# Fourteen gates of a four-branch merge computed at other places: nine beside the state space branch, two beside the last dilated group, three beside the last stick-breaking head

## The chip, the cores and the metric

The kernel runs on 1 core of one Trainium2 chip. The metric is the device time of one execution in microseconds (us), as the median of several runs.

## The reference, cut to what matters

Two transformer blocks run one after the other over 1024 positions of width 1024, all in float32. The change is in the first one, in which four mixers read the same normed input `xn` and each is gated:

```python
xn = rmsnorm(x, attn_norm_g[l])
proj = xn @ w_in[l]
...
y_pool = pool_mixer(u_pool, pool_w[l], pool_scale[l])
y_dil = dilated_attention(qkv_dil, rel_bias)
y_sb = stick_breaking_attention(qkv_sb)
y_s5 = s5_mixer(u_s5, ...)
merged = jnp.zeros_like(x)
for bi, yb in enumerate((y_pool, y_dil, y_sb, y_s5)):
    gate = jax.nn.sigmoid(xn @ w_gate[l, bi])
    merged = merged + gate * (yb @ w_branch[l, row:row + width])
x = x + merged @ w_out[l]
```

A gate depends on `xn` alone, so it can be computed at any time after the norm. Stick-breaking attention needs, for each block of scores, a log-sigmoid (absolute value, exp and ln on ScalarE), a sum over the later keys, and an exp. The state space mixer (S5) needs a convolution inside blocks of 8 positions, a recurrence over 128 blocks with sines and cosines of its angles, a gelu, and a gated linear unit (GLU).

## The kernel before, in words

It is a bare program: each engine has its own instruction list, written out in functions that end in `_pe` (TensorE), `_act` (ScalarE), `_dve` (VectorE) and `_sp` (the DMA queue of SyncE), and they meet in semaphores (`wait_ge`, `give`, and `land` for a DMA).

**Products.** A float32 product is three passes in a reduced format: the high part of the weight by the high part of the input, high by low, low by high. One product makes a tile of 128 output features by 1024 positions. `product_steps` issues it in `kt` steps of 6 matmuls of 128x512 (L417), one step for each 128 rows of the contraction; `kt` is 8 where the input is `xn`, 4 for the GLU and for most branch outputs, 2 for the dilated output. All products stand in one list, `PLAN`. With product i, SP issues the load of the weight of product i+5 (L370, which waits until the low part of weight i+2 is made), ACT makes the high part of weight i+2 (L377) and DVE its low part (L382), from rings of three buffers. Each engine must meet the products in the order of the list.

**Order of the first block.** Input and norm; S5; merge of branch 3 (S5); pool; merge of branch 0; dilated attention in three groups; merge of branch 1; stick-breaking attention in four heads; merge of branch 2; output product; FFN. A merge has for each of 8 feature tiles `ft` a gate product with a sigmoid on ACT (L1057) into a gate buffer, and a branch product (`w_br`), whose result DVE multiplies by the gate and adds into `merged`. The gate of tile ft+1 stands ahead of the branch product of tile ft. Gate (3,0) (branch 3, tile 0) is made inside S5 already.

**S5 (`s5_sp`, `s5_pe`, `s5_act`, `s5_dve`, L678 to L960).** DVE builds the kernel matrices, PE multiplies them (L727), ACT copies them to `Ks`, SP lays them out as the blocks of `Mk` with 8 DMAs (L694). Then come two halves, each of: transposes of the input tiles (L740), transposes of weights and the input products `bu`, a chain on DVE with two sines on ACT (L815, L817) up to the states `H` (L934), and two tiles `y`, each of 96 matmuls of 128x128 (L771, L773), copied by ACT (L823) and transposed (L435). At the end stand gelu, its split into high and low parts, and eight GLU products; the first of these is read by DVE in L947.

**Dilated attention and sticks.** A dilated group has 11 slots, with scores (L1298), values (L1311) and outputs (L1323). Groups 0 and 1 hold the two query products of the next group between their slots, as `side`; group 2 has no side. The results of the three groups go out and come back by DMA (L1487, `dR`) in `combine`, at the start of the merge of branch 1, after the gate products of tiles 0 and 1 and beside the first products of stick-breaking (w_in 22, 26, 30). A stick-breaking head runs over units of up to 512 columns: scores (L1602), on ACT absolute value, exp and ln (L1663, L1665, L1667), a cast of the high part (L1673), sums (L1610 to L1616), addition on DVE (L1778), exp (L1681, L1684), values (L1624). Heads 0 to 2 hold the three input products of the next head as `side`; head 3 has none. ACT preloads one table that serves both exp and ln ahead of the heads.

Of the kernel before, what the change touches and what calls it, by code (L numbers as in the profile page):

```python
# [14 lines left out]
T = 1024  # L15
# [66 lines left out]

def weight_plan():
# [17 lines left out]
    tiles("w_gate", [24], 8)  # L101
# [213 lines left out]
def build(nc, A, out, scr, spill, bsc):  # L315
    from contextlib import ExitStack
    ctx = ExitStack()
    with ctx:
# [363 lines left out]

        def s5_sp(sp):
# [6 lines left out]
            sp.e.dma_start(bsc, brow).then_inc(*land("bsc"))  # L690
            sp.wait_ge("s5_ks", 1, 1)
# [15 lines left out]
        def s5_pe(pe):  # L707
            ring = [0, 1]
            rows_ring = [0, 1]
# [3 lines left out]
            for g in range(3):  # L713
                ps = psum.take(pe, ring, f"bias{g}", ("bias_row", g))
# [3 lines left out]

            for hf in range(2):
# [10 lines left out]
            product(pe, ring, "w_in", 36, XN, ("s5_u", 2))  # L730

            for hf in range(2):
                for fl in range(2):
# [7 lines left out]
                    ins.then_inc(*give("s5_ut", f, 0))  # L741
                    ps = psum.take(pe, rows_ring, f"s5ut{f}1", ("s5_ug", f))
                    pe.wait_ge("s5_ua", f)
                    transposed(pe, ps, dst, 8, "s5_ut", f, 1)
                for n in range(2):
                    ps = psum.take(pe, rows_ring, f"s5wt{hf}{n}", ("s5_wT", hf, n))
                    pe.wait_ge("s5_w", hf, n)
                    transposed(pe, ps, work[n], 8, "s5_wt", hf, n)
                pbu = [psum.take(pe, (pA, pB)[n], f"s5bu{hf}{n}", ("s5_rot", hf)) for n in range(2)]
# [7 lines left out]
                if hf == 0:  # L757
                    product(pe, ring, "w_in", 37, XN, ("s5_u", 3))
                else:
                    product(pe, ring, "w_gate", 24, XN, ("gate", 3, 0))  # L760
                for fl in range(2):
# [14 lines left out]
                    ps = psum.take(pe, rows_ring, f"s5yt{f}", ("s5_yu", f))  # L776
                    pe.wait_ge("s5_yc", f, 1)
                    transposed(pe, ps, work[fl], 8, "s5_yt", f)
            for f in range(4):
# [3 lines left out]
        def s5_act(act):  # L783
# [6 lines left out]
            u_tile(1)  # L790
            for hf in range(2):
# [4 lines left out]
            u_tile(2)  # L796
# [2473 lines left out]
```

## Time and profile before

| | us |
|---|---|
| median of 3 runs | 3949.2 |
| lowest, highest of them | 3944.52, 3952.15 |
| the profiled execution, its own time | 3953.94 |
| its span from first to last instruction | 3952.1 |
| PE busy | 3650.9 (92%) |
| DVE busy | 1658.8 (42%) |
| ACT busy | 1126.9 (29%) |
| mean granted TensorE clock | 0.943 |

The span is cut in 40 slices on the page of the profile. PE is busy for nine tenths or more of most of them; the exceptions are the first four (input and S5, six tenths), one with the pool branch, some with dilated and stick-breaking attention, and some in the second block. A busy share of PE counts time at half clock as well; the granted clock is given beside it as a share of 2.4 GHz.

### The profile page before, as it was taken

The page shows a single profiled execution, that of the slowest core. Times are in us where ns is not written, and L with a number is a line of the kernel's source. Part 1 is how long each engine was busy: PE and PEld are TensorE (multiplying, and loading weights), DVE is VectorE, ACT ScalarE, POOL GpSimd, SP SyncE. Part 2 cuts the span into 40 slices and gives each one's busy share as a digit, 9 for nine tenths or more (in the row PEclk, how much of TensorE's full clock was granted, in tenths as well). Part 3 has the DMA queues.
Part 4 walks back from the last instruction along what each step waited for, and adds up shares of the span by engine and source line. Part 5 has one row for each costly group of instructions (what it writes and reads, how often), then busy time and mean ns, then how long its engine had stood idle before and what let it go on. Part 6 is the DMA issues. An engine that isn't in the chain of part 4 may idle for free.

```text
span 3952.1 us, 38673 instructions
## 1 busy us (share of the span) xinstructions
PE 3650.9 (92%) x16598; PEld 2948.7 (75%) x16598; DVE 1658.8 (42%) x2021; ACT 1126.9 (29%) x1563; POOL 25.2 (1%) x69
## 2 busy tenths in 40 slices
PE   6669999988999899999999979999988989999997
PEld 4558888776776588888888857788866778888785
DVE  6343342322454424333233364415763354444354
ACT  3122111333235522211111145413442151212122
POOL 0000000000000000000000000000000000000000
PEclk8669999997999899999999989999976999999998
DMA  2003232110320012111111102120011111111111
GB/s 93 14 6 107 86 107 84 43 43 29 126 78 25 8 48 96 47 50 47 50 42 54 40 30 99 54 80 28 1 38 69 38 38 48 48 48 44 52 38 53
DMA packets 74554, 210.60 MB, mean 53 GB/s; under 512 B 11640, under 2 KB 21624, under 8 KB 74368
## 3 DMA queue, kind: packets, MB, share of 16 engines
q1 hardware_dynamic: 74384, 208.14, 16.1%
q8 instruction: 131, 2.15, 0.2%
q14 instruction: 39, 0.32, 0.0%
HBM read 190.03 MB, written 16.89 MB: 52 GB/s over the span
## 4 chain that ended last, share of the span: by engine, by line
PE 82%; DVE 9%; ACT 6%; issue 1%; DMA 1%; SPq 0%; ACTq 0%; DVEq 0%
PE PS L417 69%; PE PS L429 3%; PE PS L2571 1%; PE PS L2583 1%; PE PS L773 1%; PE PS L1602 1%; PE PS L2913 1%; PE PS L1323 1%; PE PS L435 1%; DVE work L552 1%; PE PS L2910 1%; PE PS L771 1%; DVE GS L2995 1%; ACT dS L1372 1%; DVE xlo L451 1%
## 5 line engine op out<-in xcount | busy, mean ns | idle before, releaser
L417 PE MATMUL PS<-xhi,whi 128*128 128x512 f32 x3120 | 988.8, 398 | 51.3 <-DVE xlo L451 42.8
L417 PE MATMUL PS<-xlo,whi 128*128 128x512 f32 x3120 | 968.1, 392 | 0.0
L417 PE MATMUL PS<-xhi,wlo 128*128 128x512 f32 x3120 | 966.0, 391 | 0.0
L417 PEld LDWEIGHTS PS<-xhi,whi 128*128 128x128 f32 x3120 | 585.6, 190 | 192.0 <-issue 49.8
L417 PEld LDWEIGHTS PS<-xlo,whi 128*128 128x128 f32 x3120 | 590.1, 189 | 125.0
L417 PEld LDWEIGHTS PS<-xhi,wlo 128*128 128x128 f32 x3120 | 589.2, 189 | 124.8
L382 DVE TENSOR_TENSOR wlo<-raw,whi 128x1024 fp32r<-128x1024 f32 (+4 forms) x307 | 329.8, 1075 | 537.5 <-ACT whi L377 537.5
L377 ACT CAST whi<-raw 128x1024 fp32r<-128x1024 f32 (+4 forms) x307 | 284.3, 927 | 506.0 <-PE PS L417 489.8
L417 PE MATMUL PS<-fhi,whi 128*128 128x512 f32 x704 | 219.4, 393 | 8.5 <-DVE flo L451 8.5
L417 PE MATMUL PS<-flo,whi 128*128 128x512 f32 x704 | 218.2, 391 | 0.0
L417 PE MATMUL PS<-fhi,wlo 128*128 128x512 f32 x704 | 218.1, 391 | 0.0
L417 PEld LDWEIGHTS PS<-fhi,whi 128*128 128x128 f32 x704 | 133.1, 190 | 37.7 <-DVE flo L451 10.2
L417 PEld LDWEIGHTS PS<-flo,whi 128*128 128x128 f32 x704 | 133.3, 189 | 28.0
L417 PEld LDWEIGHTS PS<-fhi,wlo 128*128 128x128 f32 x704 | 133.0, 189 | 27.9
L448 ACT CAST fhi<-fuv 128x1024 fp32r<-128x1024 f32 x44 | 46.1, 1048 | 328.6 <-DVE fuv L1993 222.0
L417 PE MATMUL PS<-yhi,whi 128*128 128x512 f32 x352 | 111.1, 397 | 9.3 <-DVE ylo L451 9.3
L417 PE MATMUL PS<-ylo,whi 128*128 128x512 f32 x352 | 109.8, 394 | 0.0
L417 PE MATMUL PS<-yhi,wlo 128*128 128x512 f32 x352 | 109.7, 393 | 0.0
L2076 DVE SCALAR_TENSOR_TENSOR merged<-PS,mod,merged 128x1024 f32<-128x1024 f32 x32 | 41.1, 1284 | 151.5 <-PE PS L417 151.5
L2060 DVE TENSOR_SCALAR fcb<-fsg,V 128x1024 f32<-128x1024 f32 x44 | 35.8, 814 | 163.8 <-ACT fsg L2036 163.8
L2000 DVE TENSOR_TENSOR merged<-PS,merged 128x1024 f32<-128x1024 f32 x32 | 39.2, 1225 | 137.7 <-PE PS L417 137.7
L2036 ACT COPY fsg<-PS 128x1024 f32<-128x1024 f32 x44 | 44.8, 1018 | 174.0 <-PE PS L417 174.0
(464 smaller groups left out, 3818.8 us busy)
## 6 DMA issues: line engine op xcount, KB each, us to landing
raw<-in_w_up SPq DMA_DIRECT2D x88, 512.0 KB, 3.3
raw<-in_w_in SPq DMA_DIRECT2D x67, 512.0 KB, 3.3
adr<-in_w_ada SPq DMA_DIRECT2D x48, 512.0 KB, 4.4
raw<-in_w_gate SPq DMA_DIRECT2D x32, 512.0 KB, 3.3
raw<-in_w_down SPq DMA_DIRECT2D x32, 384.0 KB, 3.1
raw<-in_w_down SPq DMA_DIRECT2D x32, 320.0 KB, 2.9
raw<-in_w_br SPq DMA_DIRECT2D x24, 256.0 KB, 2.7
spill<-wk SPq DMA_DIRECT2D x10, 512.0 KB, 4.8
```

Source lines behind the costliest of these rows:

```text
L377: act.e.copy(whis[i % RING][:, 0:kt, :], raws[i % RING][:, 0:kt, :]).then_inc(*give("w_hi", i))
L382: dve.e.tensor_tensor(wlos[i % RING][:, 0:kt, :], raws[i % RING][:, 0:kt, :], whis[i % RING][:, 0:kt, :].bitcast(F32), ALU.subtract).then_ ...
L417: ins = pe.e.matmul(ps[:, h * 512:(h + 1) * 512], w[s][:, k, :], x[:, h * 512:(h + 1) * 512], start=(at == 0 and n == 0), stop=(at == kt - ...
L429: ins = pe.e.matmul(ps[:, h * 512:(h + 1) * 512], ones, x[:, h * 512:(h + 1) * 512], start=first, stop=last)
L435: ins = pe.e.transpose(ps[:, j * 128:(j + 1) * 128], src[:, j * 128:(j + 1) * 128], ident)
L448: act.e.copy(dst, src).then_inc(*give(*signal))
L451: dve.e.tensor_tensor(dst, src, hi.bitcast(F32), ALU.subtract).then_inc(*give(*signal))
L552: dve.e.tensor_tensor(o, a, b, op).then_inc(*dve.step())
L771: pe.e.matmul(o, Ug[:, 2 * n + gl, :], Mk[:, 2 * i + gl, :], start=True, stop=False, skip_group_check=True)
L773: ins = pe.e.matmul(o, H[m][rows, n, :], CL[m][rows, i, 1:9, :].rearrange("p a b -> p (a b)"), start=False, stop=(m == 1), skip_group_chec ...
L2036: act.e.copy(GSG[v][:, FPAD:], psum.of(j)).then_inc(*give("f2_raw", v, i))
L2076: dve.e.scalar_tensor_tensor(X1[:, ft, :], psum.of(j), gt_f(ft), X1[:, ft, :], ALU.mult, ALU.add).then_inc(*give("f2_x", c, ft))
```

## The change

A table names fourteen gates that are computed ahead of their merges (one of them, (3,0), was early before). Nine of them, with the input products w_in 36 and 37, form one stream of 11 products or 88 steps in S5. The stream is cut into slots: 10 steps ahead of the kernel products, 3 and 6 around these, one after each group of transposes, 24 steps while DVE goes from `bu` to `H` in each half, one between each tile `y` and its transposes, and 5 ahead of the GLU. Gates (1,2) and (1,4) are the side of dilated group 2; gates (2,2), (2,4) and (2,0) the side of stick-breaking head 3. Twelve of the gates are stored to the DRAM tensor `spill` (from 18 to 50 tiles) and loaded again by SP in their merge; (3,0) and (2,0) stay. The merges skip the products of these gates. Addresses and PSUM banks move to make room, and the gelu of tile f waits for tile f alone.

```diff
+EARLY_S5 = ((3, 2), (3, 4), (3, 6), (0, 0), (0, 2), (0, 4), (0, 6), (1, 0), (3, 0))
+EARLY_DIL = ((1, 2), (1, 4))
+EARLY_SB = ((2, 2), (2, 4), (2, 0))
+RESIDENT = ((3, 0), (2, 0))
+EARLY = EARLY_S5 + EARLY_DIL + EARLY_SB
...
-            if ft < 8 and (b, ft) != (3, 0):
+            if ft < 8 and (b, ft) not in EARLY:
...
+    tiles("w_gate", [8 * b + ft for b, ft in EARLY_DIL], 8)
+    tiles("w_gate", [8 * b + ft for b, ft in EARLY_SB], 8)
...
+        BESIDE = [("w_in", 36), ("w_in", 37)] + [("w_gate", 8 * b + ft) for b, ft in EARLY_S5]
+        BESIDE0 = PLAN.index(("w_in", 36, 0, 8))
+        SLOTS = [("cl", 10), ("k", 3), ("ks", 6)]
+        for hf in range(2):
+            SLOTS += [(f"ut{hf}{fl}{x}", 1) for fl in range(2) for x in range(2)] + [(f"wt{hf}{n}", 1) for n in range(2)]
+            SLOTS += [(f"turn{hf}", 8), (f"sin{hf}", 8), (f"rot{hf}", 8)]
+            SLOTS += [(f"y{hf}{fl}", 1) for fl in range(2)]
+        SLOTS += [("glu", 8 * len(BESIDE) - sum(n for _, n in SLOTS))]
...
+        def beside_pe(pe):
+            def stream():
+                for p, (name, ft) in enumerate(BESIDE):
+                    done = ("s5_u", ft - 34) if name == "w_in" else ("gate", ft // 8, ft % 8)
+                    yield from product_steps(pe, [0, 1] if p % 2 == 0 else [1, 0], name, ft, XN, done)
+
+            steps = stream()
+
+            def slot(name):
+                for _ in range(dict(SLOTS)[name]):
+                    next(steps, None)
+            return slot
...
+        def beside_act(act, slot):
+            for kind, p in slot_events(slot, 6, 2):
+                name, ft = BESIDE[p]
+                if kind == "begin":
+                    begin_act(act, name, ft)
+                else:
+                    act.wait_ge("prod", BESIDE0 + p)
+                    if name == "w_in":
+                        act.e.copy(U[:, ft - 34, :], psum.of(BESIDE0 + p)).then_inc(*give("s5_u", ft - 34))
+                    else:
+                        if p == 2:
+                            act.wait_ge("s5_cl", 1)
+                        else:
+                            act.wait_ge("gate_out", *EARLY_S5[p - 3])
+                        act.e.activation(g_early, psum.of(BESIDE0 + p), ACT.Sigmoid).then_inc(*give("gate", ft // 8, ft % 8))
...
+        def beside_sp(sp, slot):
+            for kind, p in slot_events(slot, 0, 4):
+                name, ft = BESIDE[p]
+                if kind == "begin":
+                    begin_sp(sp, name, ft)
+                elif name == "w_gate" and p < len(BESIDE) - 1:
+                    sp.wait_ge("gate", ft // 8, ft % 8)
+                    sp.e.dma_start(spill[:, 18 + ft, :], g_early).then_inc(*land("gate_out", ft // 8, ft % 8))
...
+            beside_sp(sp, "cl")
+            beside_sp(sp, "k")
             sp.wait_ge("s5_ks", 1, 1)
             sp.wait_ge("s5_mzero")
             for q in range(8):
                 sp.e.dma_start(Mk[16 * q:16 * q + 16, :, 16 * q:128], Ks[:, :, 0:128 - 16 * q]).then_inc(*land("s5_mk", q))
-            begin_sp(sp, "w_in", 36)
-            begin_sp(sp, "w_in", 37)
-            begin_sp(sp, "w_gate", 24)
+            for name, _ in SLOTS[2:]:
+                beside_sp(sp, name)
...
-            rows_ring = [0, 1]
+            rows_ring = [2, 3]
...
-                if hf == 0:
-                    product(pe, ring, "w_in", 37, XN, ("s5_u", 3))
-                else:
-                    product(pe, ring, "w_gate", 24, XN, ("gate", 3, 0))
+                for x in ("turn", "sin", "rot"):
+                    beside(f"{x}{hf}")
...
+                    beside(f"y{hf}{fl}")
+                    ps = psum.take(pe, (pA, pB)[fl], f"s5yt{f}", ("s5_yu", f))
                     pe.wait_ge("s5_yc", f, 1)
                     transposed(pe, ps, work[fl], 8, "s5_yt", f)
...
-                act.wait_ge("s5_yu", 3)
+                act.wait_ge("s5_yu", f)
...
         def merge_pe(pe, b, ys, branch=None, beside=iter(())):
             def gate(ft):
-                product(pe, dense, "w_gate", b * 8 + ft, XN, ("gate", b, ft))
+                if (b, ft) not in EARLY:
+                    product(pe, dense, "w_gate", b * 8 + ft, XN, ("gate", b, ft))
...
-                dve.wait_ge("gate", b, ft)
+                dve.wait_ge("gate_in" if (b, ft) in EARLY and (b, ft) not in RESIDENT else "gate", b, ft)
...
+            def gate(ft):
+                if (b, ft) not in EARLY:
+                    begin_sp(sp, "w_gate", b * 8 + ft)
+                elif (b, ft) not in RESIDENT:
+                    if ft - 2 >= (1 if b == 3 else 0):
+                        sp.wait_ge("merged", b, ft - 2)
+                    else:
+                        sp.wait_ge(*clear)
+                    sp.wait_ge("gate_out", b, ft)
+                    sp.e.dma_start(gate_buffer(b, ft), spill[:, 18 + 8 * b + ft, :]).then_inc(*land("gate_in", b, ft))
...
+        def early_pe(pe, ring, gates):
+            for b, ft in gates:
+                yield from product_steps(pe, ring, "w_gate", 8 * b + ft, XN, ("gate", b, ft))
...
+        def early_act(act, gates, into, clear):
+            for n, (b, ft) in enumerate(gates):
+                i = begin_act(act, "w_gate", 8 * b + ft)
+                for _ in range(7):
+                    yield
+                act.wait_ge("prod", i)
+                act.wait_ge("gate_out", *gates[n - 1]) if n else act.wait_ge(*clear)
+                act.e.activation(into, psum.of(i), ACT.Sigmoid).then_inc(*give("gate", b, ft))
+                yield
...
+        def early_sp(sp, gates, into):
+            for b, ft in gates:
+                begin_sp(sp, "w_gate", 8 * b + ft)
+                for _ in range(8):
+                    yield
+                if (b, ft) not in RESIDENT:
+                    sp.wait_ge("gate", b, ft)
+                    sp.e.dma_start(spill[:, 18 + 8 * b + ft, :], into).then_inc(*land("gate_out", b, ft))
...
-                side = queries(side_ring, g + 1) if g < 2 else iter(())
+                side = queries(side_ring, g + 1) if g < 2 else early_pe(pe, side_ring, EARLY_DIL)
...
+            act.wait_ge("gate_out", *EARLY_DIL[-1])
...
-                side = qkv(h + 1) if h < 3 else iter(())
+                side = qkv(h + 1) if h < 3 else early_pe(pe, ring, EARLY_SB)
...
+            dve.wait_ge("merged", 1, 7)
...
-        SG[2] = [tile("sg", work_at + n * TB) for n in range(2)]
+        SG[2] = [sbv, tile("sg", work_at + TB)]
```

**SyncE's queue in S5.** Rows are DMAs in the order of issue. Before, from the copy of the bias rows on:

```order
L690 DMA bsc<-brow_102 4x1152
L694 DMA Mk_105<-Ks_107 16x4096
L694 DMA Mk_105<-Ks_107 16x32x112
L694 DMA Mk_105<-Ks_107 16x32x96
L694 DMA Mk_105<-Ks_107 16x32x80
```

And in the changed kernel:

```order
L767 DMA bsc<-brow_102 4x1152
L380 DMA raw_57<-in_w_gate 128x1024
L380 DMA raw_58<-in_w_gate 128x1024
L773 DMA Mk_105<-Ks_107 16x4096
L773 DMA Mk_105<-Ks_107 16x32x112
```

Two weight loads, which before stood behind all of the `Mk` DMAs, now stand ahead of them.

**TensorE at the end of the first tile `y` of the first half.** `CL` and `H` are the output matrices and states, `work_111` is the copied tile. Before:

```order
L771 MATMUL PS<-Mk_105,Ug_108 128x128
L773 MATMUL PS<-CL_103,H_116 128x128
L773 MATMUL PS<-CL_104,H_117 128x128
L435 MATMUL PS<-ident_50,work_111 128x128 x8
```

In the changed kernel:

```order
L852 MATMUL PS<-Mk_105,Ug_108 128x128
L854 MATMUL PS<-CL_103,H_116 128x128
L854 MATMUL PS<-CL_104,H_117 128x128
L427 MATMUL PS<-xhi_65,whi_61 128x512 x2
L427 MATMUL PS<-xlo_66,whi_61 128x512 x2
L427 MATMUL PS<-xhi_65,wlo_64 128x512 x2
L445 MATMUL PS<-ident_50,work_111 128x128 x8
```

One step of a gate product now stands between the tile and its transposes.

**ScalarE in the last stick-breaking head.** Rows of one unit, late in the head. Before:

```order
L1663 ACTIVATE sbt_148_196<-PS 128x512
L1665 ACTIVATE sbt_148_196<-sbt_148_196 128x512
L1667 ACTIVATE sbt_148_196<-sbt_148_196 128x512
L1673 CAST sbhi_194<-sbt_145_193 128x384
L1684 ACTIVATE sbt_140_188<-sbt_140_188 128x256
```

In the changed kernel, with the sigmoid of a side gate (L1235) behind the unit:

```order
L1804 ACTIVATE sbt_149_197<-PS 128x512
L1806 ACTIVATE sbt_149_197<-sbt_149_197 128x512
L1808 ACT_TABLE_LOAD
L1808 ACTIVATE sbt_149_197<-sbt_149_197 128x512
L1814 CAST sbhi_195<-sbt_146_194 128x384
L1825 ACT_TABLE_LOAD
L1825 ACTIVATE sbt_141_189<-sbt_141_189 128x256
L1235 ACT_TABLE_LOAD
L1235 ACTIVATE sbv_177<-PS 128x1024
```

Where no table was loaded inside a head before, one is now loaded ahead of each ln and each exp that follow the first sigmoid: 22 loads in this head.

## Rows read from the trace of the kernel before

**Rows 1.** The page: the chain that ended last, share by engine.
```profile
PE 82%; DVE 9%; ACT 6%; issue 1%; DMA 1%; SPq 0%; ACTq 0%; DVEq 0%
```

**Rows 2.** Busy time by stretch: stretch, us, PE, PEld, DVE, ACT, POOL busy, PEclk, DMA, GB/s.
```profile
134.30:157.60 23.30, 0.02 (x1) 0.05 (x1) 19.46 (x28) 2.91 (x3) 0.00 (x0) 0.57 0.00 0
157.60:193.50 35.90, 33.43 (x113) 26.14 (x114) 2.09 (x1) 2.15 (x4) 0.00 (x0) 0.50 0.00 1
331.80:453.00 121.20, 121.20 (x552) 100.90 (x551) 47.27 (x46) 23.85 (x27) 0.00 (x0) 1.00 0.36 119
930.50:973.70 43.20, 30.80 (x169) 27.24 (x169) 21.92 (x42) 18.56 (x74) 0.00 (x0) 0.57 0.10 22
1319.80:1372.90 53.10, 36.22 (x103) 19.88 (x102) 26.34 (x49) 30.28 (x63) 5.36 (x16) 0.81 0.00 0
```

**Rows 3.** Timeline, PE, two product starts in merge 3: start, us, engine, what.
```profile
331.75 0.62 PE L417 MATMUL PS<-xhi,whi 128*128 128x512 f32 x2
...
342.63 0.62 PE L417 MATMUL PS<-yhi,whi 128*128 128x512 f32 x2
```

**Rows 4.** The page: DMA issues, the spill stores, KB each and us to landing.
```profile
spill<-wk SPq DMA_DIRECT2D x10, 512.0 KB, 4.8
```

**Rows 5.** Timeline, SP's queue in S5: the eight DMAs of Mk.
```profile
93.80 13.11 SPq L694 DMA_DIRECT2D Mk<-Ks  x8
```

**Rows 6.** Timeline, DVE in S5; in brackets the idle time before and its releaser.
```profile
108.80 1.23 DVE L552 TENSOR_TENSOR work<-PR,Br 128x1024 f32<-128x1024 f32 x1 [12.78 <-DMA Mk<-Ks]
...
293.87 1.23 DVE L947 COPY U<-PS 128x1024 f32<-128x1024 f32 x1 [1.97 <-PE PS L417]
```

**Rows 7.** Timeline, PE in S5: the tiles y of both halves, first transposes.
```profile
157.58 0.77 PE L771 MATMUL PS<-Mk,Ug 128*128 128x128 f32 x2 [23.32 <-DVE H L934]
...
173.92 1.94 PE L435 MATMUL PS<-ident,work 128*128 128x128 f32 x8 [1.31 <-ACT work L823]
...
243.58 0.77 PE L771 MATMUL PS<-Mk,Ug 128*128 128x128 f32 x2 [24.39 <-DVE H L934]
```

**Rows 8.** Stretches in the second block, PE line L2901: us, PE busy, PEclk, DMA, GB/s.
```profile
2948.20:2952.80 4.60, 3.64 (x14) 1.00 0.00 0
2956.00:2972.00 16.00, 16.00 (x43) 0.50 0.00 0
```

**Rows 9.** Timeline, PE: start of dilated group 1, its end, end of group 2.
```profile
822.67 0.72 PE L1298 MATMUL PS<-K,Qs 64*128 64x128 f32 x8
...
878.35 1.21 PE L417 MATMUL PS<-xhi,whi 128*128 128x512 f32 x2 [0.52 <-DVE dO L1444]
...
973.69 1.22 PE L417 MATMUL PS<-xhi,whi 128*128 128x512 f32 x2 [0.52 <-DVE dO L1444]
```

**Rows 10.** Timeline, SP's queue, DVE and PE at the start of merge 1.
```profile
990.87 4.95 SPq L1487 DMA_DIRECT2D dR<-scr  x3
...
1004.45 0.19 DVE L552 TENSOR_TENSOR dM<-dR 128x32 f32<-128x32 f32 x1 [14.59 <-DMA dR<-scr]
...
1021.33 0.83 PE L417 MATMUL PS<-xhi,whi 128*128 128x512 f32 x2 [2.09 <-DVE wlo L382]
```

**Rows 11.** Timeline, PE: starts of stick-breaking heads 2 and 3.
```profile
1257.58 1.04 PE L435 MATMUL PS<-ident,sbv 128*128 128x128 f32 x8
...
1319.82 1.04 PE L435 MATMUL PS<-ident,sbv 128*128 128x128 f32 x8
```

**Rows 12.** Timeline, ACT: a table load in S5, two units of head 3, merge 2.
```profile
220.27 1.28 ACT L815 ACT_TABLE_LOAD   x1
221.56 1.06 ACT L815 ACTIVATE work<-work 128x1024 f32<-128x1024 f32 x1
...
1361.94 0.63 ACT L1684 ACTIVATE sbt<-sbt 128x512 f32<-128x512 f32 x1 [1.45 <-DVE sbt L1778]
...
1367.00 0.63 ACT L1684 ACTIVATE sbt<-sbt 128x512 f32<-128x512 f32 x1 [1.45 <-DVE sbt L1778]
...
1374.25 1.28 ACT L1057 ACT_TABLE_LOAD   x1 [0.28 <-DVE ylo L451]
```

More of the change, by code:

```diff
@@ L100, in weight_plan @@
     tiles("w_in", range(34, 38), 8)
-    tiles("w_gate", [24], 8)
+    tiles("w_gate", [8 * b + ft for b, ft in EARLY_S5], 8)
     tiles("w_glu", [x for i in range(4) for x in (i, i + 4)], 4)
@@ new lines, in build, with slot_events @@
+        SLOTS += [("glu", 8 * len(BESIDE) - sum(n for _, n in SLOTS))]
+        def slot_events(slot, begin_late, end_late):
+            at = 0
+            for name, n in SLOTS:
+                first, last = at, at + n
+                at = last
+                if name == slot:
+                    break
+            last = last if slot != "glu" else 1000
+            first = first if slot != "cl" else -1
+            events = [(8 * p + begin_late, "begin", p) for p in range(len(BESIDE))] + [(8 * p + 7 + end_late, "end", p) for p in range(len(BESIDE))]
+            return [e[1:] for e in sorted(events) if first <= e[0] < last]
@@ L708, in s5_pe @@
             ring = [0, 1]
-            rows_ring = [0, 1]
+            rows_ring = [2, 3]
+            beside = beside_pe(pe)
             pA, pB = [2], [3]
@@ L729, in s5_pe @@
                 ins.then_inc(*give("s5_kmm", hf))
-            product(pe, ring, "w_in", 36, XN, ("s5_u", 2))
+                beside("ks" if hf else "k")
             for hf in range(2):
@@ L744, in s5_pe @@
                     transposed(pe, ps, dst, 8, "s5_ut", f, 1)
+                    beside(f"ut{hf}{fl}1")
                 for n in range(2):
@@ L807, in s5_act @@
                     act.e.copy(WT[n], v8(psum.of(f"s5wt{hf}{n}"))).then_inc(*give("s5_wT", hf, n))
-                if hf == 0:
-                    u_tile(3)
-                else:
-                    i = begin_act(act, "w_gate", 24)
-                    act.wait_ge("prod", i)
-                    act.e.activation(g_early, psum.of(i), ACT.Sigmoid).then_inc(*give("gate", 3, 0))
+                    beside_act(act, f"wt{hf}{n}")
                 act.wait_ge("s5_turn", hf, 0)
@@ L890, in s5_dve @@
                 dve.e.tensor_tensor(wi, wi, wt, ALU.add).then_inc(*give("s5_w", hf, 1))
-                if hf == 0:
-                    begin_dve(dve, "w_in", 37)
-                else:
-                    begin_dve(dve, "w_gate", 24)
+                for fl in range(2):
+                    beside_dve(dve, f"ut{hf}{fl}0")
+                    beside_dve(dve, f"ut{hf}{fl}1")
+                for n in range(2):
+                    beside_dve(dve, f"wt{hf}{n}")
                 S, Cc, P, Q, R = work
@@ L1220, in build @@
         Vf = mem("Vf", y_at + 29184, [128, 2, T])
+        dil_gate = tile("dgate", y_at + 29184)
         Vt = mem("Vt", y_at + 37376, [128, 8, 256])
@@ L3128, in scalar @@
             sb_act(act)
[L3129 removed]
+            merge_act(act, 2, ("ysb_lo", 3, 1), done=merged_hi)
             out_act(act)
@@ L3150, in vector @@
             sb_dve(dve)
-            merge_dve(dve, 2, done=early_dve)
+            merge_dve(dve, 2, done=merged_lo)
             last_square = out_dve(dve)
```

80 lines of the change are left out of this document (54 added, 26 removed).

## The prediction

> **What bounds the kernel now.** I read the chain of waits first: 82% of the time that set the end is on PE, 9% on DVE, 6% on ACT [rows 1]. So most product time counts in full, but there are places where another engine leads. The busy time by stretch shows which [rows 2]. In merge 3 PE is busy for 121.20 of 121.20 us at full clock, with DVE at 47.27 and ACT at 23.85: a product less there is its whole time less. Three other stretches have room on PE. Before the first tile y of S5 PE does nothing for 23.3 us while DVE works for 19.46 of them. In dilated group 2 PE is busy for 30.80 of 43.2 us, in the last stick-breaking head for 36.22 of 53.1, in both partly at half clock (0.57 and 0.81 granted). The timelines then give the length of a product and the waits at the ends of these stretches.
>
> A gate product is 342.63 - 331.75 = 10.88 us at full clock, so a step is 1.36 us [rows 3].
>
> **The change part by part.** The sum is made against the profiled execution, 3953.9 us, which is 4.7 above the median of the runs.
>
> *Merges.* Gate (3,0) was early already, so 13 gate products leave the merges: 13 x 10.88 = 141.4 us less. Twelve loads of gates come in, with 4.8 us of flight for a tile of 512 KB as the stores have it [rows 4]. SP waits for the merge two tiles back before it issues one, and behind it queue weight loads for products five ahead, so they keep several products of cover. DVE and ACT keep their work and stay below PE: merge 3 becomes 121.2 - 3 x 10.9 = 88.6 us long with under 47.3 of DVE. I add 3 us for small stalls; bounds 0 (all covered) and 12 (1 us at each load).
>
> *S5, head.* SP issues two weight loads ahead of the eight `Mk` DMAs [rows 5]; the second waits for a low part that DVE makes in this stretch. DVE idles 12.78 us for `Mk` until 108.80 [rows 6], so a delay of `Mk` passes on. Bounds: 0, and one product period, 10.9. I take 5. From 108.80 to the last input product is 14.6 us before (157.58 - 23.32 - 10.88 = 123.4) [rows 7]; six single steps come in between transposes, of which most fall into waits of 1 to 2 us there. I add 2.6: `bu` ends at 131.0.
>
> *S5, the two stretches of 24 steps.* 24 x 1.36 = 32.6 us. Before, one product and the idle time behind it took 10.88 + 23.32 = 34.2 and 10.88 + 24.39 = 35.3 [rows 7]. DVE's chain hides under the steps; what PE's steps cost here is nothing, and they end a little before or with DVE. First tiles y at 163.6 instead of 157.6.
>
> *S5, tiles y.* A tile took 173.92 - 1.31 - 157.58 = 15.0 us at half clock [rows 7], with 33.43 of 35.9 us busy and a granted clock of 0.50 [rows 2]. PE now comes to them at full clock, from 32.6 us of dense products. Does it keep it? The nearest case is in the second block: small matmuls at 1.00 for 4.6 us, then 0.50 over 16.00 us in which PE was busy for 16.00 [rows 8]. So unbroken work of this kind did not hold the clock. I take the same: in the first 4.6 us at full clock 61% of a 7.5 us tile is done, the rest takes 5.8, so 10.4 for the first tile and 15.0 for the second; behind each one step (2.7 at half clock) and transposes (1.94). A pair: 10.4 + 15.0 + 2 x 4.7 = 34.8, against 35.9. The Trainium skill (TensorE: Matmul & The Clock Gate, Why this matters for your kernels) asks for no PE-idle gaps between bursts so that the clock stays up; by it the tiles would take 7.5 us each here, since PE has no gap before them. Rows 8 speak against that; it is rival B.
>
> *S5, to the end.* First pair ends at 198.4 (193.5 before). To the end of the second `bu` 14.6 us, plus 4.1 for six steps less the waits that they fill: 217.1; 24 steps: 249.7 (before 243.58); pair: 284.5; five steps, some at half clock, 8: 292.5, under which gelu and its split run; half a product, 5.4. The read of the first GLU product comes at 297.9 instead of 293.87 [rows 6]: **+4**. So the eight gates that are new here cost 4 us together.
>
> *Dilated group 2.* Group 1, with two side products, took 878.35 - 822.67 = 55.7 us, group 2 without them 43.2 [rows 9], which has 12.4 us of idle PE and a low clock. Two products are 21.8 us of PE at full clock: 30.8 + 21.8 = 52.6 if nothing ran faster, less what the higher clock gives back. I take 50: **+7** (bounds +4 and +12.5, the length of group 1).
>
> *Merge 1, head.* PE comes to product 30 at 1021.33, 47.6 us after the merge's start, with a wait of 2.09; DVE had waited 14.59 for `dR` and then worked 15.5 us on the combination before its weight parts [rows 10]. Without gate (1,0) PE is there at 36.8, but this chain does not shorten by itself. `dR` is issued at 17.2 us after the start now; I put it at 8 to 12, since ACT first waits for the last gate store (4.8 us [rows 4]). 10 + 13.6 + 15.5 + 1.4 = 40.5: **+4** of the 10.9 given back (bounds 0 and 10.9).
>
> *Stick-breaking head 3.* Three gates come in beside the units. Head 2, with three side products, took 1319.82 - 1257.58 = 62.2 us [rows 11], head 3 53.1: +9.1 by that alone. But a sigmoid replaces the table that held exp and ln, and the order shows 22 table loads after it where none was. A load is 1.28 us [rows 12]. ACT leads the units: 5.06 us each, with 1.45 idle, for DVE, before the last exp [rows 12]. The load ahead of that exp runs before the wait (as the load at 1374.25 ran ahead of its sigmoid's wait), so nine of them are hidden in 1.45 us each; if DVE were faster they would show. The eight ahead of ln and the five around the sigmoids are exposed: 13 x 1.28 = 16.6. Together 62.2 + 16.6 = 78.8: **+26** (bounds +9 with all hidden, +37 with all 22 exposed). The Trainium skill (ScalarE: Activation LUTs, What ACT_TABLE_LOAD costs) puts a switch at 2.66 us with a drain; by it 22 switches would be 58.5, the head 121 and the whole 29 us above case C. In the trace the sine follows its load at once (220.27 + 1.28 = 221.55, start 221.56), so I see no drain.
>
> *Moved addresses, banks, the gelu's wait for its own tile:* nothing; the DVE wait for the last tile of merge 1 stands before a memset whose work the first head needs only after it.
>
> Sum: -141.4 + 3 + 4 + 7 + 4 + 26 = -97.4, or 3856.5 for this execution; with 4.7 off for the median, **3852**.
>
> **The rivals.**
> *A, the forecast*, 3852, own range 3840 to 3866 by the bounds above taken together.
> *B, the clock holds in the tiles y.* Then a tile is 7.5 and step and transposes 2.4: a pair 19.8, 15 less, twice: 30 less, 3822. For it: PE has not one wait ahead of the tiles any more, and at 157.6 it came out of 23 us of nothing. Against it: rows 8.
> *C, all 22 loads exposed*: +37 instead of +26, 3863. For it: ACT already leads the units; against it: the waits of 1.45.
> *D, the clock is low through the dense steps of S5.* Waits on weights or on stores of gates (the next sigmoid waits for the store of the last, and PE's bank for that sigmoid) break the stream, and it runs at 1.2 GHz. A step is 2.72 then; 88 steps cost 120 us more, and the change is slower than before (3852 + 120 = 3972). It decides at 97.4 / 1.36 = 72 of 88 steps. Against it: merge 3 holds 1.00 with the same instructions and the same weight chain [rows 2].
> *E, the early gates stall their stages a little everywhere* (SP's queue in S5, PE waiting for a bank): 10 to 25 us, 3862 to 3877. The change does what it says: the order shows the gates at their new places.
>
> **How the numbers follow.** A 0.52, B 0.2, C 0.12, D 0.03, E 0.13. The likeliest is A: 3852. The range goes from a B with a little lost (3815) to E's end with C (3880). A measurement of this kernel can tell about 0.2% (8 us) from no change. All cases but D are faster by far more: faster 0.96, same 0.01, slower 0.03.
>
> **What would show it.** The granted clock in the two tile stretches (0.5 to 0.7: A; 1.0: B). PE busy without a break in two stretches of 32.6 us ahead of them. The `Mk` DMAs at 94 to 105. 22 table loads in head 3 and a length of 79 us, against 90 for C. Group 2 at 50. An idle of PE ahead of the third stick-breaking product in merge 1 of some 4 to 6 us. Merges with PE busy throughout. Wrong I would be most if head 3 or the tiles y came out otherwise, as they carry 26 and 30 us; if merges showed PE waiting for gate loads, the first term falls.

## The result, and the profile after

| | before | changed |
|---|---|---|
| median, us | 3950.16 (4 runs) | 3830.07 (4 runs) |
| lowest to highest | 3944.52 to 3952.15 | 3829.21 to 3833.62 |
| span of the profiled execution | 3952.1 | 3831.9 |
| mean granted clock | 0.943 | 0.964 |
| PE busy | 3650.9 (92%) | 3604.6 (94%) |

The ratio is 0.970, with a 95% interval of 0.9685 to 0.9714: 120 us faster. The forecast was 3852 with a range of 3815 to 3880, so the time is inside it, but 22 us under the value that was named, and the way there was partly another one.

The spans differ by 120.2 us. Set against each other at the same points of the two traces (ends of adds, of heads, of groups), they give:

| stretch | before, us | changed, us | difference | forecast |
|---|---|---|---|---|
| up to the read of the first GLU product | 293.87 | 276.15 | -17.7 | +4 |
| from there to the end of merge 3 (3 gates) | 162.67 | 130.05 | -32.6 | -32.6 |
| pool and merge 0 (4 gates) | 186.11 | 142.61 | -43.5 | -43.5 |
| dilated groups 0 and 1 | 235.18 | 233.17 | -2.0 | 0 |
| dilated group 2 with its products | 95.34 | 103.60 | +8.3 | +7 |
| merge 1 (3 gates) | 161.33 | 136.01 | -25.3 | -32.6 + 4 |
| stick-breaking heads 0 to 2 | 185.32 | 185.51 | +0.2 | 0 |
| head 3 | 53.0 | 80.4 | +27.4 | +26 |
| merge 2 (3 gates) | 133.13 | 100.49 | -32.6 | -32.6 |
| all behind it | 2446.1 | 2443.9 | -2.3 | 0 |

The ten gates of merges 3, 0 and 2 gave their full price, 10.88 us each, with no stall. The forecast had also 3 us for small stalls in the merges.

The busy time by stretch of the changed kernel, in the columns of [rows 2]: the first stretch of 24 steps in S5, the two pairs of tiles y, dilated group 2, the part of merge 1 from its first multiply on, and head 3.

```profile
128.40:161.20 32.80, 32.80 (x147) 27.16 (x146) 24.89 (x34) 8.71 (x9) 0.00 (x0) 1.00 0.28 79
161.19:182.94 21.75, 21.75 (x125) 16.78 (x123) 2.07 (x1) 3.08 (x5) 0.00 (x0) 1.00 0.07 28
235.31:256.91 21.60, 21.60 (x126) 17.09 (x125) 2.07 (x1) 4.40 (x7) 0.00 (x0) 1.00 0.00 1
834.90:885.58 50.68, 42.98 (x259) 34.77 (x258) 23.69 (x42) 24.92 (x79) 0.00 (x0) 0.93 0.13 40
944.29:1021.60 77.31, 72.13 (x318) 59.74 (x316) 46.46 (x47) 12.63 (x16) 0.00 (x0) 0.93 0.53 182
1207.10:1287.50 80.40, 65.79 (x246) 45.24 (x245) 29.58 (x52) 63.92 (x90) 5.42 (x16) 0.94 0.08 27
```

The largest surprise is in the second and third row: where the clock was 0.50 for 35.9 us [rows 2], it is now 1.00, and a pair takes 21.7 us instead of 36. PE has no idle time in it. Group 2 now takes 50.68 us; before, up to the same point, it was 42.7. In merge 1 a clock of 0.93 and 5.2 us of idle PE stand where it was 1.00. In head 3 ACT is busy for 63.92 of 80.40 us.

The timelines show the waits. On SP and DVE the start behind the `Mk` DMAs, with the columns of [rows 5] and [rows 6]:

```profile
70.17 28.14 SPq L380 DMA_DIRECT2D raw<-in_w_gate  x2
98.43 13.26 SPq L773 DMA_DIRECT2D Mk<-Ks  x8
```
```profile
113.46 1.23 DVE L562 TENSOR_TENSOR work<-PR,Br 128x1024 f32<-128x1024 f32 x1 [15.46 <-DMA Mk<-Ks]
...
276.15 1.23 DVE L1039 COPY U<-PS 128x1024 f32<-128x1024 f32 x1 [1.87 <-PE PS L427]
```

DVE goes on 4.66 us later than before (113.46 for 108.80), where 5 was forecast.

On PE: the first GLU product, the third stick-breaking product in merge 1, and the matmuls that finish the condition vector:

```profile
267.68 1.19 PE L427 MATMUL PS<-yhi,whi 128*128 128x512 f32 x2 [3.96 <-DVE ylo L461]
...
921.66 0.87 PE L427 MATMUL PS<-xhi,whi 128*128 128x512 f32 x2 [3.34 <-DVE wlo L392]
...
967.15 3.57 PE L1109 MATMUL PS<-ones,ada 128*128 128x1 f32 x16 [3.86 <-DVE ada L1085]
```

The first wait was 5.65 us before, but without five steps of other work ahead of it; the second was 2.09 [rows 10]; the third is new. All three leave PE at half clock for a while: a pair of 128x512 matmuls takes 1.19 us behind the first, for 0.62 at full clock [rows 3], and 1.05 and 1.20 behind the other two.

On ACT, one unit late in head 3:

```profile
1268.16 1.28 ACT L1808 ACT_TABLE_LOAD   x1
1269.45 0.64 ACT L1808 ACTIVATE sbt<-sbt 128x512 f32<-128x512 f32 x1
...
1270.61 1.28 ACT L1825 ACT_TABLE_LOAD   x1
1272.04 0.63 ACT L1825 ACTIVATE sbt<-sbt 128x512 f32<-128x512 f32 x1
...
1274.51 1.28 ACT L1808 ACT_TABLE_LOAD   x1
```

A unit takes 1274.51 - 1268.16 = 6.35 us, for 5.06 before [rows 12]: one load more, not two. The load ahead of the exp fills the former wait for DVE (1.45 us), as forecast. The ln starts right behind its load (1.29 us after the load's start, for 1.28 of load); this exp comes 0.15 us later, as its wait outlasts the load by that much. ACT's busy time in the head has 22 loads in it.

### The profile page after: what moved, and what is told of

Its sections match the earlier page's. It is cut to its first block, busy times and chain, and to the rows that moved or that the text cites. A ratio compares the mean times of both kernels' runs of the same rounds, so it can differ in the third digit from the quotient of the medians.

```text
span 3831.9 us, 38735 instructions
## 1 busy us (share of the span) xinstructions
PE 3604.6 (94%) x16598; PEld 2913.9 (76%) x16598; DVE 1658.3 (43%) x2021; ACT 1161.2 (30%) x1588; POOL 25.2 (1%) x69
## 4 chain that ended last, share of the span: by engine, by line
PE 83%; DVE 8%; ACT 7%; DMA 1%; issue 1%; SPq 0%; ACTq 0%; DVEq 0%
PE PS L427 69%; PE PS L439 2%; PE PS L2725 1%; PE PS L2713 1%; PE PS L3055 1%; PE PS L1743 1%; PE PS L445 1%; PE PS L3052 1%; ACT dS L1511 1%; PE PS L1462 1%; PE PS L1765 1%; PE PS L854 1%; DVE xlo L461 1%; DVE GS L3137 1%; PE PS L2718 0%
## 5 line engine op out<-in xcount | busy, mean ns | idle before, releaser
L392 DVE TENSOR_TENSOR wlo<-raw,whi 128x1024 fp32r<-128x1024 f32 (+3 forms) x307 | 329.9, 1076 | 471.2 <-ACT whi L387 471.2
L387 ACT CAST whi<-raw 128x1024 fp32r<-128x1024 f32 (+3 forms) x307 | 284.9, 929 | 514.6 <-PE PS L427 490.5
L427 PEld LDWEIGHTS PS<-fhi,whi 128*128 128x128 f32 x704 | 133.1, 190 | 37.7 <-DVE flo L461 10.2
L2202 DVE TENSOR_SCALAR fcb<-fsg,V 128x1024 f32<-128x1024 f32 x44 | 35.8, 814 | 163.6 <-ACT fsg L2178 163.6
```

The source lines that it names most:

```text
L387: act.e.copy(whis[i % RING][:, 0:kt, :], raws[i % RING][:, 0:kt, :]).then_inc(*give("w_hi", i))
L392: dve.e.tensor_tensor(wlos[i % RING][:, 0:kt, :], raws[i % RING][:, 0:kt, :], whis[i % RING][:, 0:kt, :].bitcast(F32), ALU.subtract).then_ ...
L427: ins = pe.e.matmul(ps[:, h * 512:(h + 1) * 512], w[s][:, k, :], x[:, h * 512:(h + 1) * 512], start=(at == 0 and n == 0), stop=(at == kt - ...
```

## The experiments

All are edits of the changed kernel, and are held against its 3830.1. The times of equal stages vary by some us from run to run: in merge 1 from its first multiply on, the unaltered code took 73.8 to 77.3 us in different kernels. Its traces show why. PE waits 2.85 to 3.86 us for the condition vector there; the clock falls at that wait each time, but it stays at half for 3.4 us in the traces with 73.8 to 74.0 us and for 6.8 to 10.2 us in the others. The program of the changed kernel gave both (77.3, and 73.8 in e11, which has the same instructions). Dilated group 2 with its products, 103.6 us in the changed kernel, took 98.8 to 104.2 with unaltered code. So a single stage is read from the traces, and a difference of a few us in these two is within what equal code does.

### Head 3: tables or TensorE

Run e1_raw_sb, where the sigmoid of the three gates (`RAW = EARLY_SB`) is taken in merge 2:

```diff
 # early_act, for the gates of head 3
...
-act.e.activation(into, psum.of(i), ACT.Sigmoid).then_inc(*give("gate", b, ft))
+if (b, ft) in RAW:
+    act.e.copy(into, psum.of(i)).then_inc(*give("gate_raw", b, ft))
+else:
+    act.e.activation(into, psum.of(i), ACT.Sigmoid).then_inc(*give("gate", b, ft))
...
 # merge_act, at the place of the gate
+if (b, ft) in RAW:
+    act.wait_ge("gate_raw" if (b, ft) in RESIDENT else "gate_in", b, ft)
+    act.e.activation(gate_buffer(b, ft), gate_buffer(b, ft), ACT.Sigmoid).then_inc(*give("gate", b, ft))
```

> The three gates beside stick-breaking head 3 are stored as plain products (a copy on ScalarE, which needs no table) and their sigmoids are taken in merge 2. No table is loaded inside head 3. Theory T (the table loads are what head 3 pays beyond the 62.2 us of a head with side products): head 3 falls from 80.4 to 62.2 us, time 3830 - 18 = 3812. Rival P (TensorE's side steps and the one PSUM pair that they share with the transposes hold the units back): head 3 stays at 75 us or more, 3825 or more. Merge 2 should not change under either.

Measured: 3810.85 us (ratio to before 0.9645, 0.9631 to 0.9660). Head 3 by stretch:

```profile
1199.60:1262.00 62.40, 59.33 (x246) 43.04 (x245) 29.45 (x52) 35.30 (x68) 5.34 (x16) 1.00 0.10 34
```

The same 246 matmuls take 62.4 us instead of 80.4, ACT's 63.92 us are 35.30, and the clock is 1.00 instead of 0.94. The 28.6 us of ACT that went are 22 x 1.28 with the difference of three copies. This is theory T; P is refuted. Merge 2 took 100.5 us as before the edit.

Run e2_preload puts the table back behind each sigmoid:

```diff
 act.e.activation(into, psum.of(i), ACT.Sigmoid).then_inc(*give("gate", b, ft))
+if b == 2:
+    act.e.preload_act_table_set("natural_log_exp_and_others")
```

> After each of the three sigmoids in head 3 the table that serves both exp and ln is loaded again; 6 loads instead of 22. Theory T with every load ahead of ln exposed: 8 x 1.28 = 10.2 us less, head 3 at 70, time 3820. If all of ScalarE's loads count once it is the busiest engine there, 16 x 1.28 = 20.5 less but not below 62.2 + 3 x 2.56 = 69.9, the same. Rival P: within 3 us of 3830.

Measured: 3820.98 us (0.9667, 0.9652 to 0.9681), head 3 at 73.2 us. The time is as T has it; the head is 3 us longer than the 70 that were expected. So the 16 loads that went are worth 7.2 us, not 10.2, and the six that are left beside the sigmoids cost 10.8 (73.2 - 62.4), more than the 7.7 us that they last.

Run e3_no_sb takes the three gates out of head 3:

```diff
-EARLY_SB = ((2, 2), (2, 4), (2, 0))
-RESIDENT = ((3, 0), (2, 0))
+EARLY_SB = ()
+RESIDENT = ((3, 0),)
```

> Undoes the three gates in head 3; all else as changed. The merge gets 3 x 10.88 = 32.6 us back, head 3 falls from 80.4 to 53.0 us (27.4 less): 5 slower than the changed kernel, 3835. If the gates cost something outside head 3 too (stores, the loads in merge 2), the time is under 3835; if they saved more than their products there, over it.

Measured: 3835.11 us (0.9704, 0.9688 to 0.9720). So three gates that save 32.6 us in merge 2 are worth 5 us with the sigmoids in the head, and 24 with the sigmoids left out of it (3835.1 - 3810.9).

### The clock in the tiles y

The trace of the changed kernel cannot tell whether the clock stays up because PE comes from dense products, or because of the step behind each tile. Three runs complete a table of two by two.

```diff
 # e4_gap: 8 of the 24 steps ahead of each pair are moved behind the tiles, ahead of the GLU
-            SLOTS += [(f"turn{hf}", 8), (f"sin{hf}", 8), (f"rot{hf}", 8)]
+            SLOTS += [(f"turn{hf}", 8), (f"sin{hf}", 8), (f"rot{hf}", 0)]
```

> The last 8 of the 24 steps ahead of the tiles y of each half are moved behind the tiles, to the slot ahead of the GLU. TensorE then idles some 7 us ahead of each pair of tiles. Theory G (the clock in the tiles is what TensorE brings with it; an idle time ahead of them loses it and the small matmuls don't win it back): granted clock 0.5 to 0.6 in the tiles, a pair 34 to 36 us instead of 21.7, time 3830 + 2 x 14 + 9.6 = 3868. Rival S (the step between the tile and its transposes holds the clock up, whatever was before): clock near 1.00, 2 x 4.1 us earlier at the tiles, 16 steps or 21.8 us later, 4 of them in an idle time: 3840.

Measured: 3855.42 us (0.9758, 0.9743 to 0.9772), between the two theories. The stretches are the first and the second tile of each pair, the timeline is PE's:

```profile
157.14:172.10 14.96, 14.96 (x48) 11.37 (x49) 0.00 (x0) 0.00 (x0) 0.00 (x0) 0.50 0.00 0
175.10:186.80 11.70, 11.70 (x64) 9.35 (x63) 2.06 (x1) 1.07 (x2) 0.00 (x0) 0.91 0.01 1
237.33:252.30 14.97, 14.97 (x49) 11.38 (x49) 0.00 (x0) 0.00 (x0) 0.00 (x0) 0.50 0.00 1
255.20:266.20 11.00, 11.00 (x65) 8.74 (x64) 2.07 (x1) 1.53 (x3) 0.00 (x0) 0.98 0.01 1
```
```profile
157.14 0.77 PE L852 MATMUL PS<-Mk,Ug 128*128 128x128 f32 x2 [6.88 <-DVE H L1023]
...
172.10 1.22 PE L427 MATMUL PS<-xhi,whi 128*128 128x512 f32 x2
...
185.13 0.74 PE L427 MATMUL PS<-xhi,whi 128*128 128x512 f32 x2
```

After 6.88 us of idle PE the first tile runs at 0.50 throughout, although PE is busy for all of its 14.96 us. The one step behind it begins at half clock (1.22), and behind step and transposes the second tile is at full clock, in the first pair after 0.6 us of it. Each theory had one half right.

```diff
 # e5_yout: the single steps behind the tiles are moved ahead of the GLU
-            SLOTS += [(f"y{hf}{fl}", 1) for fl in range(2)]
+            SLOTS += [(f"y{hf}{fl}", 0) for fl in range(2)]
```

> The four single steps between a tile y and its transposes are moved to the slot ahead of the GLU; the 24 dense steps ahead of each pair stay. Theory G (the tiles keep the clock that TensorE brings; 1.3 us of wait ahead of the transposes don't lose it): granted clock near 1.00 in both pairs, a pair 19 to 21 us, the end within 4 us of the changed kernel, 3826 to 3833. Rival S (only the steps in between hold it): the second tile of each pair at half clock, a pair 27 to 29, time 3842 or more.

Measured: 3843.14 us (0.9718, 0.9700 to 0.9737); of its four executions one was at 3830.38 and three at 3841.7 to 3848.3. Rival S. In the profiled one:

```profile
161.90:171.60 9.70, 8.46 (x49) 6.41 (x48) 0.00 (x0) 0.84 (x2) 0.00 (x0) 0.98 0.16 63
173.70:191.50 17.80, 16.64 (x57) 12.76 (x56) 2.09 (x1) 1.07 (x2) 0.00 (x0) 0.50 0.00 0
246.20:255.80 9.60, 8.41 (x49) 6.41 (x47) 0.00 (x0) 1.07 (x2) 0.00 (x0) 1.00 0.20 77
256.90:274.50 17.60, 16.44 (x56) 12.78 (x56) 2.10 (x1) 2.64 (x4) 0.00 (x0) 0.50 0.00 0
```

The first tile of each pair keeps the clock that PE brings, the second has lost it. The time of 3830.38 would fit an execution in which it was kept: its mean granted clock is 0.964, that of the other three 0.958 to 0.960. It has no trace.

Run e6_gap_yout has both edits.

> Both edits together: some 7 us of idle TensorE ahead of each pair, and no step behind a tile. In the run with the gap alone the first tile took 15 us at half clock and the second 8.4 at full, behind one step. If the clock comes back through that step, both tiles are at half clock here, a pair 34 to 36 us as before the change, and the time is some 5 us over the run with the gap alone (3855): 3860. If it comes back by itself in the transposes, a pair stays at 30 and the time at 3853.

Measured: 3877.93 us (0.9811, 0.9796 to 0.9825), 18 us over the expected 3860: the pairs came out as expected at half clock, but the second tiles, some 6 us longer in each pair, were left out of my sum. They are 12 of the 18 us; of the rest 3 lie between the pairs, and the others were not followed up.

```profile
156.20:192.20 36.00, 33.61 (x112) 25.94 (x112) 2.08 (x1) 2.15 (x4) 0.00 (x0) 0.50 0.00 1
245.05:281.00 35.95, 33.57 (x113) 26.26 (x114) 2.09 (x1) 4.05 (x6) 0.00 (x0) 0.50 0.00 0
```

These are the rows of the kernel before [rows 2]. So the table is:

| | no step behind a tile | one step behind each tile |
|---|---|---|
| 6.4 to 8.5 us idle ahead | half, half: 36.0 us | half, then full: 30 us |
| dense steps up to the tile | full, then half: 29 to 30 us | full, full: 21.7 us |

The two parts of the change that matter are the filled idle time and the single step. Each one alone leaves one tile of a pair at 1.2 GHz.

What the step does is not settled by that: it puts 128x512 matmuls behind the tile, and it also fills the wait ahead of the transposes, which in e5 is 1.53 and 1.22 us. The traces narrow it down. In the same execution of e5, later, PE waits as long behind 128x512 matmuls alone, and the clock stays at 1.00:

```profile
171.89 1.97 PE L445 MATMUL PS<-ident,work 128*128 128x128 f32 x8 [1.53 <-ACT work L906]
...
255.83 1.27 PE L445 MATMUL PS<-ident,work 128*128 128x128 f32 x8 [1.22 <-ACT work L906]
...
3213.01 0.73 PE L427 MATMUL PS<-fhi,whi 128*128 128x512 f32 x2 [1.46 <-DVE flo L461]
```
```profile
3211.50:3220.00 8.50, 7.04 (x32) 5.79 (x32) 4.24 (x4) 1.77 (x3) 0.00 (x0) 1.00 0.33 93
```

Over all traces there are 44 waits of 1.2 to 1.6 us behind a run of 128x512 matmuls alone, and the clock fell at one of them (in e10, 1002.29). And no tile that began at full clock lost it within its 8.4 us without a break. So the tile alone never took the clock and such a wait alone hardly ever; the wait behind the tile did in both pairs of e5. For the way back to full clock a filled wait is not enough: 15 us of tile without a break stayed at 0.50 (e4).

### The end of S5 and merge 1

Run e7_glu_order moves DVE's weight part behind the low parts of the gelu:

```diff
-            beside_dve(dve, "glu")
             for f in range(4):
                 dve.wait_ge("gx_hi", f)
                 lo_of(dve, Y[1][:, f, :], U[:, f, :], Y[0][:, f, :], "gx_lo", f)
+            beside_dve(dve, "glu")
```

> VectorE makes the low parts of the gelu's four tiles ahead of its weight part of the last slot, which waits for ScalarE's weight part behind all four gelus. Theory: the 3.96 us in which TensorE waits for the first GLU product go, and the half clock of its first matmuls with them: 4 to 5 us less, 3825.5. Rival (the gelu chain on ScalarE ends as late anyway): under 1.5 us less.

Measured: 3822.21 us (0.9668, 0.9653 to 0.9682). PE works on from the last transposes without a break, and the first multiply of merge 3 comes at 325.07 us instead of 330.55, 5.5 earlier. The medians differ by 7.9; the rest is not in this stage, and merge 1 from its first multiply on happened to take 74.0 us here.

Run e8_dil_26 takes another pair of gates for dilated group 2:

```diff
-EARLY_DIL = ((1, 2), (1, 4))
+EARLY_DIL = ((1, 2), (1, 6))
```

> The two gates beside dilated group 2 are (1,2) and (1,6) instead of (1,2) and (1,4); the number of products stays. Merge 1 gave back 8.5 us of the 21.8 that these two gates free from its first multiply on: TensorE waits 3.86 us for the condition vector that VectorE sums up, and goes on at half clock for a while. Theory V (VectorE has too much to do in the first half of this merge): the wait goes, 5 to 8.5 us less, 3822 to 3825. Rival D (the loads of gates and of the condition weights compete, whatever the place): within 2 us of 3830.

Measured: 3823.59 us (0.9674, 0.9658 to 0.9691), the time and the wait as theory V has them; D is refuted. From the first multiply of merge 1 on:

```profile
939.85:1009.17 69.32, 68.00 (x318) 56.51 (x317) 46.56 (x47) 12.62 (x16) 0.00 (x0) 0.99 0.55 191
```

With the same 318 matmuls, 69.3 us instead of 77.3 (73.8 to 77.3 with unaltered code), and no wait on `ada`. That is 90.5 - 69.3 = 21.2 of the 21.8 us of two gates. But V's reason, that DVE has too much to do, is not what the traces show. DVE has the same 46.5 us to do in both, and ends the eighth and last addition to the vector 22.8 us after the first multiply in the changed kernel and 22.0 here. In the changed kernel it even idles for 4.1 us on the way, 3.6 of them behind loads of condition weights, for example:

```profile
951.20 1.28 DVE L1085 SCALAR_TENSOR_TENSOR ada<-adr,cond,ada 128x1024 f32<-128x1024 f32 x1 [2.26 <-DMA adr<-in_w_ada]
...
965.81 1.28 DVE L1085 SCALAR_TENSOR_TENSOR ada<-adr,cond,ada 128x1024 f32<-128x1024 f32 x1 [1.11 <-DMA adr<-in_w_ada]
```

What moved is PE: it comes to the condition matmuls 19.0 us after the first multiply in the changed kernel, 30.3 us after it here, because the product of gate (1,4) stands ahead of them again and that of (1,6) is taken away behind them. A chain of some 22 us through DMA and DVE does not shorten with PE's products; whether DVE or the loads set its length was not tried.

Run e12_no_dil undoes the pair:

```diff
-EARLY_DIL = ((1, 2), (1, 4))
+EARLY_DIL = ()
-            act.wait_ge("gate_out", *EARLY_DIL[-1])
```

> Undoes the two gates beside dilated group 2; all else as changed. Two products come back to merge 1, 21.8 us; group 2 falls back by the 8 to 9 us that they cost it, and merge 1 loses its wait for the condition vector, 8.5 us less: 4 to 5 us slower than the changed kernel, 3834.5. If the wait stays although the gates are back, it is not theirs: 3843.

Measured: 3833.49 us (0.9704, 0.9690 to 0.9718). The wait is gone, and that part of merge 1 is at 90.5 us, as before the change. So the two gates were worth about 3 us as placed; this is within what runs differ by. With e8's choice they are worth 10 (3833.5 - 3823.6).

### A run that changed nothing, and the sum

Run e11_mk_first was to put the `Mk` DMAs ahead of one more weight load:

```diff
             beside_sp(sp, "cl")
-            beside_sp(sp, "k")
...
-            for name, _ in SLOTS[2:]:
+            for name, _ in SLOTS[1:]:
```

> In SP's queue the eight Mk DMAs go ahead of the weight load that waits for a low part; all else as changed. They start when the Ks copies end, 2.5 us earlier, and VectorE goes on 2.5 us earlier after them: 2 to 3 us less, 3827.5, if that chain sets the end there. If TensorE's steps set it (they fill 24 of 33 us without a break), nothing.

Measured: 3831.05 us (0.9695, 0.9681 to 0.9708), and no earlier `Mk`:

```profile
70.91 28.15 SPq L380 DMA_DIRECT2D raw<-in_w_gate  x2
99.18 13.62 SPq L772 DMA_DIRECT2D Mk<-Ks  x8
```

Both weight loads still stand ahead: they belong to the slot in front, and the slot that I moved holds none of SP's work. So this is the changed kernel once more, and says that two sets of runs agree within 1 us. What an earlier `Mk` would bring was not tried.

Run e9_all has e1, e7, e8 and that empty edit together.

> The four edits that point to a gain together: plain products stored beside head 3 (19 less by run e1), VectorE's order at the end of S5 (8 less by its median, 5.5 by the trace), gates (1,2) and (1,6) beside dilated group 2 (6.5), and the Mk DMAs ahead of one more weight load (2.5, not measured yet). If they add up: 3830 - 19 - 6 - 6.5 - 2.5 = 3796, give or take 3. If two of them share a wait: above 3802.

Measured: 3800.40 us (0.9618, 0.9605 to 0.9632). Without the 2.5 us of the `Mk` edit 3798.5 was expected: the three add up within the 3 us that were allowed. By the medians of the single runs (19.2, 7.9 and 6.5) they would have come to 3796.5. Head 3 took 62.33 us at clock 1.00, merge 1 from its first multiply on 68.7. This version beats the changed kernel by 29.7 us and the kernel before by 151.

Run e10_all_raw_dil adds the gates beside group 2 to those stored as plain products (`RAW = EARLY_SB + EARLY_DIL`).

> As the run before, and the two gates beside dilated group 2 are stored as plain products as well, with the sigmoid in merge 1. Three or four table loads of 1.28 us and the sigmoid's place leave group 2. Theory: 2 to 5 us less than the run before. Rival: in merge 1 ScalarE now waits for the load of the gate ahead of its weight parts, where a branch product lasts 2.7 us only, and TensorE waits behind it: 0 to 8 us more.

Measured: 3805.20 us (0.9632, 0.9618 to 0.9645), 4.8 more than e9: the rival. Merge 1 from its first multiply on took 72.8 us for 68.7, and PE has a wait for the condition vector again:

```profile
1002.29 1.92 PE L1109 MATMUL PS<-ones,ada 128*128 128x1 f32 x16 [1.56 <-DVE ada L1085]
```

Group 2 took 101.1 us for 101.9, a smaller difference than equal code shows from trace to trace, so this does not tell what its table loads cost. What holds the vector up in merge 1 (ACT's weight parts behind the load of a gate, as the rival has it) the trace does not single out.

## Why the prediction was right or wrong

*Merges: right to the tenth where PE alone led.* PE busy 121.20 of 121.20 us was all the evidence that was needed. "DVE and ACT keep their work and stay below PE" failed in merge 1: its branch products have two steps (2.7 us), and condition work is woven in, whose vector is ready 22.8 us after the first multiply, while PE, with a gate product less, comes to it after 19.0. I read the room from merge 3, whose branch products have four steps and which has no such chain, and carried it over. It gave back 7.3 us, where 4 at its head and a share of 3 were forecast; the head itself gave back nothing that can be seen (first multiply 11.4 us earlier, counted from the merge's first product, for 10.88 of gate), since `dR` was issued 6.2 us after the merge's start, not 8 to 12.

*S5: the step that failed is "I take the same: in the first 4.6 us at full clock 61% of a 7.5 us tile is done, the rest takes 5.8".* It cost 26 us of forecast: pairs of 34.8 were measured at 21.7 and 21.6. The reading under it was wrong: [rows 8] shows two stretches, at 1.00 and at 0.50, and "unbroken work of this kind did not hold the clock" skips what lies between them. There PE idled:

```profile
2952.80:2956.00 3.20, 0.75 (x2) 0.50 (x2) 3.00 (x6) 0.00 (x0) 0.00 (x0) 0.64 0.02 5
```
```profile
2955.25 17.92 PE L2901 MATMUL PS<-gv,kdt 64*128 64x256 f32 x44 [2.46 <-DVE GS L2995]
```

The clock fell in that wait of 2.46 us, not in unbroken work. It is the same order as in e5, where the first tile runs 8.4 us at 1.00 and the clock falls about the wait behind it, so that only the second tile is at half. I also had the step of dense matmuls behind each tile in hand, but priced it only as 2.7 us of work and gave it no effect on the clock. Rival B said 3822; the 8 us that lack to it are in S5 too (276.15 for the 267.9 that it gives for the read of the first GLU product): a pair is 21.7 and not 19.8, as a tile takes 8.4 us at full clock and not half of 15.0, and from the second pair to that read it is 19.2 us for 13.4, with the first GLU product waiting 3.96 us and running at half clock, which no case had. The cause of that wait is DVE's weight part ahead of the gelu's low parts (e7). S5 was forecast 21.7 us too long, which is nearly all of the 22 us between the named value and the median. That the other errors leave almost nothing is luck: 3 us of stalls did not come and the stages that nobody touched took 4.1 us less, while merge 1 took 3.3 us more than forecast, head 3 1.4 and group 2 1.3.

*The idle time that was filled* is a cause as well: e4 costs 25.3 us, of which the moved work accounts for the 9.6 that were worked out ahead of it; the two pairs together took 17 us longer. The Trainium skill (TensorE: Matmul & The Clock Gate, Why this matters for your kernels) asks for no idle gaps between bursts of matmuls; the first tiles agree (0.50 behind 6.88 us of idle, 1.00 behind dense steps), the second tiles of e5 show that filling the long gap was not enough here.

*The two stretches of 24 steps: right.* 32.8 and 32.9 us, at clock 1.00, with DVE's chain underneath; first tiles at 161.2 for 163.6. `Mk` came 4.66 us later, for 5.

*Group 2: right in size*, +8.3 for +7, though equal code differs by 5 us there. *Head 3: right in cause and total*, +27.4 for +26, by loads exposed ahead of ln and hidden ahead of exp; the split was another one, 18.0 us for the loads as a whole instead of 16.6, of which those about the sigmoids took more and those ahead of ln less (e2). The 2.66 us a switch of the Trainium skill (ScalarE: Activation LUTs, What ACT_TABLE_LOAD costs) would, by an estimate, have made a unit 2 x 2.66 - 1.45 = 3.9 us longer; it got 1.3 longer, so the measurement decides against the drain here. By the same price the whole would have been 30 us above case C (58.5 - 28.2), where the prediction has 29.

*Open:* groups 0 and 1 took 2.0 us less and all behind merge 2 took 2.3 less, neither touched by the change in its code and neither followed up. No run has a tile behind dense steps, no step behind it and no wait either, so that the clock in e5 falls by tile and wait together is read from the rows above and not tested alone. The text ahead of the prediction gives a tile `y` 96 matmuls of 128x128; the traces record 48 a tile, 16 of them over 128 rows and 32 over 64.

## What to carry to other kernels

Work that fills an idle time of the matrix engine is priced too low if only its own time is counted: look which small matmuls come right behind it and at which clock they run, and put a few dense matmuls between stretches of sparse ones, above all where a wait stands there. Before a row is taken as a model of the clock, look at the idle time between its stretches. Before a function goes into a stage of ScalarE, list the tables that the stage uses; if it needs another, move the plain value and apply the function where its table is loaded already (19 us for three gates here). And check the room in each stage that gets shorter, not in the one that looks like it: where a chain on another engine ends in the middle of the stage, take away products that stand behind that point (e8: 6.5 us less for the same number of gates).

## What the runs showed of the hardware that was not expected

- Tiles of 48 recorded matmuls with 128 columns each ran at either clock, 8.4 or 15 us, by what stood ahead of them. At half clock, 15 us of unbroken such matmuls did not bring the full clock back (e4: 0.50 over 14.96 us with PE busy for 14.96); six matmuls of 128x512 and eight transposes behind them (4.6 us in the first pair) did, while the transposes alone did not (e6).
- With dense steps ahead and 1.2 to 1.5 us of wait behind the tile, one and the same program (e5) had one time of 3830.4 and three of 3841.7 to 3848.3, wider than any other kernel here. The mean granted clocks, 0.964 against 0.958 to 0.960, go with it, so a stage that loses the clock in some executions only is the likely cause; the fast one has no trace.
- Every fall of the clock in the traces here has idle time of PE close ahead of it; the least is 0.92 us, in e5 behind a tile.
